# Eight state updates moved to other places in the job list of a decoder step

## The reference

```
h = rms_norm(x) * (1 + scale) + shift
q, k, v, fl, z, xbc, dt, ga, gb = split(h @ w_in)
o_att = forgetting_attention(q, k, v, ...)            # branch A
y_ssm, ssm_new = mamba2_branch(z, xbc, dt, ssm0, ...) # branch B
m = sigmoid(ga) * (o_att @ w_pa) + sigmoid(gb) * (y_ssm @ w_pb)
x = x + gate1 * (m @ w_o)
x = x + gate2 * grouped_moe(rms_norm(x) * ...)        # 16 experts, top 2
```

## Time and profile before

| | us |
|---|---|
| median of 3 runs | 771.57 (770.38 to 772.34) |
| the profiled execution | 770.76 |
| its span | 769.2 |
| PE busy | 727.5 (95%) |
| DVE busy | 382.6 (50%) |
| ACT busy | 285.0 (37%) |
| POOL busy | 99.2 (13%) |

### The profile page before, as it was taken

How to read it: one execution, slowest core, us unless ns; L and a number is a source line. 1 busy time by engine, 2 the same in 40 slices (tenths; PEclk the granted TensorE clock), 3 DMA queues, 4 the chain that set the end, 5 groups by cost and what they waited for, 6 DMA issues and landing times.

```text
span 769.2 us, 12251 instructions
## 1 busy us (share of the span) xinstructions
PE 727.5 (95%) x4419; PEld 499.0 (65%) x4419; DVE 382.6 (50%) x963; ACT 285.0 (37%) x670; POOL 99.2 (13%) x169
## 2 busy tenths in 40 slices
PE   3899998999999989999989989999999999999987
PEld 3475687778785668788868878887634344434434
DVE  1364337777674088798999211112423343324324
ACT  3221157656775123668885000012513122212201
POOL 4331021122110113620100100000010000000000
PEclk9999999999999999999999989999999999999999
DMA  9997364979786621359999595567899999999992
GB/s 316 331 344 227 116 205 153 331 232 322 241 300 186 216 60 57 114 158 390 365 318 333 197 397 203 163 259 296 320 411 422 416 421 422 416 421 421 419 413 80
DMA packets 90126, 219.46 MB, mean 285 GB/s; under 512 B 12982, under 2 KB 57238, under 8 KB 76622
## 3 DMA queue, kind: packets, MB, share of 16 engines
q1 hardware_dynamic: 73360, 181.71, 64.3%
q0 software_dynamic: 7840, 31.67, 12.1%
q10 hardware_dynamic: 8862, 5.25, 2.3%
HBM read 207.07 MB, written 13.22 MB: 286 GB/s over the span
## 4 chain that ended last, share of the span: by engine, by line
PE 56%; SPq 12%; DMA 9%; DVE 9%; ACT 6%; issue 4%; POOL 2%; POOLq 1%; ACTq 1%; DVEq 0%
PE bank L1786 15%; PE bank L2023 8%; SPq L599 8%; PE bank L2115 6%; PE bank L2031 4%; PE bank L2140 4%; SPq L597 3%; PE bank L1779 3%; PE bank L2007 3%; DMA conv_out<-in_w_mod 3%; DMA arena<-in_w_up 3%; PE bank L1696 3%; PE bank L1736 2%; DMA arena<-in_state_ssm 2%; DVE arena L1473 2%
## 5 line engine op out<-in xcount | busy, mean ns | idle before, releaser
L1786 PE MATMUL bank<-h_normed,weight_ring 128*128 128x264 f32 x1024 | 239.0, 390 | 3.2 <-ACT conv_work L1091 3.2
L1786 PEld LDWEIGHTS bank<-h_normed,weight_ring 128*128 128x128 f32 x1024 | 192.1, 191 | 39.1 <-issue 4.2
L2023 PE MATMUL bank<-y_T,weight_ring 128*128 128x264 f32 x256 | 60.6, 400 | 2.5 <-DVE y_T L1510 2.5
L2115 PE MATMUL bank<-arena,h_normed 128*64 128x512 f32 x136 | 60.3, 594 | 0.0
L2023 PEld LDWEIGHTS bank<-y_T,weight_ring 128*128 128x128 f32 x256 | 50.4, 198 | 11.7 <-issue 2.6
L1596 DVE TENSOR_TENSOR arena<-arena,bank 128x512 f32<-128x512 f32 x8 | 8.4, 1052 | 84.6 <-PE bank L2115 84.6
L1696 PE MATMUL bank<-identity,arena 128*128 128x128 f32 (+5 forms) x218 | 30.4, 281 | 14.0 <-ACT arena L904 9.8
L1083 ACT ACTIVATE arena<-conv_out,early_small 128x128 f32<-128x128 f32 x128 | 38.3, 387 | 11.1 <-DVE arena L1473 10.4
L873 POOL DMA_INDIRECT h_normed<-h_scratch,token_rows x7 | 7.1, 1020 | 252.6 <-DVE token_rows L1563 135.1
L2140 PE MATMUL bank<-arena 128*64 128x512 f32 x88 | 39.2, 595 | 0.0
L1395 DVE SCALAR_TENSOR_TENSOR conv_work<-conv_work,conv_out 128x288 f32<-128x288 f32 x72 | 37.7, 524 | 2.5
(11 more groups left out here) (404 smaller groups left out, 1212.0 us busy)
## 6 DMA issues: line engine op xcount, KB each, us to landing
weight_ring<-in_w_in SPq DMA_DIRECT2D x36, 1024.0 KB, 6.2
weight_ring<-in_w_mod SPq DMA_DIRECT2D x22, 1024.0 KB, 10.2
arena<-in_w_down SPq DMA_DIRECT2D x11, 1024.0 KB, 23.8
arena<-in_w_gate SPq DMA_DIRECT2D x10, 1024.0 KB, 13.8
weight_ring<-in_w_down SPq DMA_DIRECT2D x10, 1024.0 KB, 14.4
weight_ring<-in_w_up SPq DMA_DIRECT2D x9, 1024.0 KB, 24.9
arena<-in_state_ssm POOLq DMA_DIRECT2D x8, 1024.0 KB, 11.2
out_ssm_sample<-arena POOLq DMA_DIRECT2D x8, 1024.0 KB, 8.5
```

What stands on the lines that cost most here:

```text
L1786: ins = mm(ps[:, 0:T], w, hT[:, c, :], start=c == 0, stop=c == KD - 1)
L2023: ins = mm(ps[:, 0:T], w, yT[:, c, :], start=c == 0, stop=c == NXB - 1)
L2115: ins = mm(banks[i][BLK * e:BLK * e + BLK, :], xg[:, 4 * h + c, BLK * e:BLK * e + BLK], ws[e][c], start=h == 0 and c == 0, stop=h == 1 and ...
```

## The change

The list of the merge is made by putting the four normalisations among the gates and then the eight updates among both. Before, update i stands ahead of the job with index 2i of that merged list, so the updates stand ahead of g0, g1, yp1, g4, g5, yp3, g8 and g10. Now a list names the jobs: g0, g2, g4, g7, g10, g12, g14 and pa0.

```diff
         merge = [("g", i) for i in range(16)] + [("pa", i) for i in range(8)]
         for g in range(SG):
             merge.insert(1 + 3 * g, ("yp", g))
-        for i, j in enumerate(merge):
-            if i % 2 == 0 and i // 2 < NS:
-                jobs += [("ssm", i // 2)]
+        ahead_of = [("g", 0), ("g", 2), ("g", 4), ("g", 7), ("g", 10), ("g", 12), ("g", 14), ("pa", 0)]
+        for j in merge:
+            if j in ahead_of:
+                jobs += [("ssm", ahead_of.index(j))]
             jobs += [j] + ([("ys",)] if j == ("pa", 6) else [])
```

## The result

The changed kernel took 776.19 us (median of 20 runs) against 771.99 for the kernel before (20 runs). The ratio is 1.0056, 95% interval 1.0040 to 1.0072: slower by about half a per cent, where 771.3 and no change were forecast, and outside the stated range (767.6 to 774.6).

The account below looks back on a forecast made before the run. It blamed TensorE's 3.23 us stall for a PSUM bank ScalarE empties late, then the sample outputs' round trip. 0.5 us later from VectorE's order and 0.8 back from the clock gave -0.3 on 771.57: 771.3 us, range 767.6 to 774.6.

Parts of the forecast that it names:

- VectorE's new order, walked: VectorE's updates and state loads: update 7 ends at 427.5, 4.15 us later; the sample norm's matmul starts 0.5 us later.
- the round trip: Sample outputs stored and fetched back by DMA: with updates ending at 427.5, they land at 440.2.
- TensorE's stall: TensorE's 3.23 us wait before 399.42 for a PSUM bank goes; TensorE could reach the sample norm at 435.1, 5.7 earlier.
- the gates' cover: ScalarE empties the gates' PSUM banks in time for TensorE, with more than 10 us to spare; waits costed at nothing.
- The ceiling of 3.6 us: Were VectorE's updates to end at 423.35 as before, the sample norm's matmul could start at 437.2, 3.6 us earlier.
- Update 3 at 387.9: On VectorE, normalisations 2 and 3 now precede update 3, which starts at 387.9 instead of 380.88, 7.0 us later.
- Load 6: State load for update 6: issued at 401.2 behind store 3, takes 12.2 us, lands at 413.4; VectorE waits 1.85.
- Load 7 in time: State load for update 7: issued behind stores 4 and 5, takes 11.0 us, lands at 419.2, so VectorE doesn't wait.
- The clock behind "yn": TensorE's first 32 matmuls after the sample norm's matmul start slowly again, costing 2.3 us, a gain of 0.8.
- B: Rival: state loads stay at 14.4 us, load 7 lands at 423.3; 775.0, or 774.2 with the clock's 0.8; chance 0.18.
- A: Rival: state loads run fast, VectorE waits 0.6 in all, the sample norm's matmul comes 3.2 earlier; 767.6 us; chance 0.23.
- C: Rival: the stall goes but nothing comes of it, because the expert weights set the end; 771.6 us; chance 0.04.

Follow-up runs that it names:

- e3: Changed kernel, with SyncE fetching the weights of branch-B slabs 2 to 5 only once the sample rows are back: 768.09 us, ratio 0.9956 to the kernel before.
- e9: Changed kernel, branch-B slabs 2 to 5 held until sample rows return, second half of branch A's weights until sample 5's state lands: 764.62 us, ratio 0.9932.
- e1: The kernel before, run once more unedited for a second profile: 771.6 us.
- e2: The changed kernel, run once more unedited for a second profile: 775.93 us.
- e5: Changed kernel with VectorE's order of before and the weights of branch-B slabs 2 to 5 held until the sample rows return: 765.18 us, ratio 0.9918.
- e8: Changed kernel with only the weights of branch-B slabs 4 and 5 held until the sample rows are back: 770.37 us, ratio 0.9994.
- e6: Kernel before, with the weights of branch-B slabs 2 to 5 held until the sample rows are back: 771.17 us, ratio 1.0002.
- e4: Changed kernel with VectorE's part of the normalisations put back behind updates 0, 2, 3 and 5, ScalarE keeping the changed order: 767.55 us, ratio 0.9958.

## Why the prediction was wrong

**The step that failed** is in "VectorE's new order, walked": "Update 7 ends at 427.5, which is 4.15 later than now. The outputs land at 440.2". That is 12.7 us for the round trip, because it took so long before. It took 15.5. The mechanism around it held, and a term was mis-sized: 12.7 was no property of a store and a fetch of 64 KB, but of what SyncE moved beside them (2.47 MB; 4.08 after the change; 0.02 in e3, where it takes 8.3). The prediction had the cause in hand and priced it at nothing. It had TensorE 5.7 us ahead of the old time, and didn't ask which weights the freed places would let in. Of SyncE's weights it said that they go out later and "are wanted at 444", not what they would collide with; that is true of the first place alone, which keeps its distance to the trip, while the weights of the second and third place come earlier against it.

The other steps, one by one:

- TensorE's stall: right. None is left but 0.44 us of another kind, and it is through at 88.0 behind gate 0, 435.8 on the scale of before (435.1 forecast). Gates 7 to 9 are emptied at 388.72 - 2.71 = 386.0 on that scale (387), and the gates' cover held.
- The ceiling of 3.6 us, if the updates ended as before: right by its parts. 4.76 (updates) + 2.85 (trip) - 3.6 is 4.0, and "yn" came 97.08 - 92.98 = 4.1 later.
- Update 3 at 387.9: 390.77 - 2.71 = 388.1. Load 5 issued at 391.2, taking 13.3: 391.4 and 13.1, a wait of 2.44 (2.5 forecast).
- Load 6: issued at 399.3 on that scale, not at 401.2, since the store ahead of it took 7.9 us and not 9.9; but it took 14.7, not 12.2. The wait was 2.47 instead of 1.85. Both errors nearly cancel, which is luck. e9 shows that the branch weights beside it make up much of the load's time (8.0 us with them held, 15.3 in e3).
- Load 7 in time: right, by 0.4 us (412.24 + 11.16 = 423.40, update 7 at 423.77). The updates end 4.76 later, 4.15 forecast.
- "yn" to the first `pb` slab: not in the sum. It takes 2.39 us instead of 3.42 (from 440.78 to 444.20 before), as ScalarE now loads the root's table at 422.91, ahead of "yn", and before it loaded it behind "yn", for 1.28 us. A gain of 1.0.
- The clock behind "yn": 0.8 forecast. The 32 matmuls took 9.82 us and not 10.28: 0.46 back. But e1, the same kernel as before, took 9.04, and the slowest execution of the changed kernel 8.88, so no effect of the change shows in them. The prediction set the Trainium skill beside it, page "TensorE: Matmul & The Clock Gate", section "Part 1: The HAM clock gate": the slow start of one kernel differs from run to run. The traces agree: 10.28 and 9.04 us in two executions of the kernel before, 9.82 and 8.88 in two of the changed one.

With the trip at 12.7 the sum from gate 0 to the end of those 32 matmuls would be -3.6 + 4.76 - 1.0 - 0.5 = -0.3, the forecast. That it comes out so exactly is luck: the updates were 0.6 later than forecast, the clock gave back 0.3 less, and the 1.0 of "yn" to the first slab, which was in no sum, made up for both. With the trip as measured it is 109.29 - 106.68 = 2.6 (449.98 + 9.82 - 350.51, and 444.20 + 10.28 - 347.80). Against e1, where the same stretch took 105.47, it is 3.8. The medians differ by 4.2, the interval of the ratio says 3.1 to 5.6. Nothing more is lost behind the merge: from the end of the 32 matmuls to the end of the span it takes 314.6 us in e2, 314.7 in the profile of before and in e1, and 313.3 to 315.2 in all eleven profiles. So at most 3 us are not located, and single executions, which begin gate 0 anywhere from 347.8 to 351.4 us, can't settle them.

**The rivals.** B (774.2 to 775.0) came nearest, but its mechanism is not what happened: load 7 didn't wait, and the time was lost behind the updates. Its condition, that load 6 lands after update 5 has ended, was met (416.7 against 414.3), but so it is in the forecast's own walk, so it doesn't tell the two apart. A's condition, fast loads, was not met; e9 met it for loads 5 and 6 and lost the gain at load 7. C did not decide: e3 to e5 gain through to the end, and what follows the merge takes about the same time in all eleven profiles.

## What to carry to other kernels

A transfer's duration read from a trace includes what moved beside it. When a change lets an engine free its buffers earlier, ask which transfers that starts, and price every small transfer on the critical path that they will meet; here a 64 KB fetch cost 3.7 to 7.9 us by that alone. If such a meeting can't be avoided by order, one wait on the queue of the large transfers buys it back (e3, e8), but only where the small transfer is what is late (e6 gained nothing).

And a move in a shared list moves the work on every engine: the stall needed ScalarE's order alone, and undoing VectorE's half (e4) kept the gain without the price.

## What the runs showed of the hardware

**Most of a slow fetch's delay lies ahead of its first packet.** In the changed kernel, in 438.3 to 443.3, 1663 packets of SyncE's queue moved and none of the fetch. The last piece of that fetch, 443.3 to 446.4:

```profile
q1 hardware_dynamic: 646, 0.66, 103.2%
q0 software_dynamic: 48, 0.07, 8.7%
```

and the quiet one in e3, first 435.8 to 437.7, then 437.7 to 439.6:

```profile
DMA packets 0, 0.00 MB, mean 0 GB/s; under 512 B 0, under 2 KB 0, under 8 KB 0
...
q0 software_dynamic: 48, 0.07, 38.6%
```

All 48 packets of the fetch lie in the second piece in both. With the engines empty the first comes about 1.9 us behind the issue; with SyncE's queue full about 5. Once it moves it is slowed too, but by less: the 48 packets lie within 1.3 us in e3 and within 2.3 us here. In the kernel before, no packet of the fetch moves in 429.7 to 433.8 (SyncE's queue at 109.3%), and the first come as that share falls, 87.1% in 433.9 to 434.0. In the changed kernel they came with it still at about 100%, so its falling is no condition for them. The Trainium skill, page "DMA: Bandwidth & Descriptors", section "Queues, rings and completion order", says that an engine takes turns between queues, packet by packet. By that a fetch would be slowed once it moves; the trace puts the larger part of the delay ahead of its first packet, which the rule doesn't explain and no run here takes apart.

**An issue can take 8.25 us.** ScalarE's fourth store of a stretch did, in one of the eleven profiles; the same instruction took 0.39 to 0.40 in nine others and 1.23 in e9. What brought it on was not tried. SyncE's queue has such an issue as well: the fourth of the `pb` weights took 5.28 us in the changed kernel (at 426.39), and at most 0.97 us in the kernel before.
